# Norm chains between w_o and the feed-forward moved to the other half of PSUM, sums in two parts, two feed-forward chapters of h0 in a row

## The reference, cut to what matters

```python
y = hybrid_mixer(...)                      # its last step is  concat @ w_o
x = x + g1 * rms_norm_2(y, mix_post_g)     # "residual 3"
h = rms_norm_2(x, ffn_pre_g) * (1 + sc2) + sh2   # "apply 4"
g, u = split(h @ w_ffn_in)
y = (silu(g) * u) @ w_ffn_out              # D_FF = 2816 hidden channels
x = x + g2 * rms_norm_2(y, ffn_post_g)     # "residual 5"
```

## Time and profile before

| what | value |
|---|---|
| median of 3 runs | 2596.87 us (2590.79 to 2598.59) |
| the profiled execution's own time | 2598.15 us |
| its span | 2595.5 us (2.65 us lie around it) |
| mean granted TensorE clock | 0.946 of full speed |
| TensorE busy | 2337.8 us, 90% |
| VectorE, GpSimd, ScalarE busy | 1438.1, 1371.8, 819.5 us |

### The profile page before, as it was taken

One profiled execution on the slowest core, in us unless ns is written; L12 is line 12 of the kernel. 1 busy time (PEld: TensorE's weight loads), 2 busy tenths in 40 slices (PEclk: granted clock), 3 DMA queues, 4 the chain that ended last, 5 costly groups with the idle time before them and its releaser, 6 DMA issues. The chain is left out here.

```text
span 2595.5 us, 32228 instructions
## 1 busy us (share of the span) xinstructions
PE 2337.8 (90%) x11279; PEld 1926.6 (74%) x11279; DVE 1438.1 (55%) x2168; ACT 819.5 (32%) x1454; POOL 1371.8 (53%) x1332
## 2 busy tenths in 40 slices
PE   6898998999999999898788968797899999999995
PEld 2687888788887787776557846675678878888874
DVE  1743646577663999758789667648632212222236
ACT  3531113034213888623234257524320000000012
POOL 2545556652344887275369856575653833333360
PEclk9899999999998999898899979898999999999997
DMA  7435444423365565152223567452221311111121
GB/s 272 146 114 163 126 136 137 162 66 110 118 198 167 159 172 154 53 183 66 98 75 114 162 178 232 159 182 61 73 78 49 113 47 49 49 49 49 49 65 65
DMA packets 179725, 304.86 MB, mean 117 GB/s; under 512 B 34860, under 2 KB 73448, under 8 KB 178288
## 3 DMA queue, kind: packets, MB, share of 16 engines
q1 hardware_dynamic: 137760, 217.51, 28.9%
q10 hardware_dynamic: 41808, 85.31, 8.9%
HBM read 246.09 MB, written 56.66 MB: 117 GB/s over the span
## 5 line engine op out<-in xcount | busy, mean ns | idle before, releaser
L950 POOL TENSOR_SCALAR WH<-RAW 128x512 fp32r<-128x512 f32 (+1 forms) x462 | 344.2, 745 | 974.0 <-PE PS L1063 828.7
L1061 PE MATMUL PS<-HXH,WH 128*128 128x512 f32 (+1 forms) x1904 | 761.9, 400 | 74.5 <-ACT TM L1717 14.9
L1062 PE MATMUL PS<-HXL,WH 128*128 128x512 f32 (+1 forms) x1904 | 752.7, 395 | 0.0
L1063 PE MATMUL PS<-HXH,WL 128*128 128x512 f32 (+1 forms) x1904 | 751.6, 395 | 0.0
L953 POOL TENSOR_TENSOR WL<-RAW,WH 128x512 fp32r<-128x512 f32 (+1 forms) x462 | 632.1, 1368 | 38.5
L1061 PEld LDWEIGHTS PS<-HXH,WH 128*128 128x128 f32 (+1 forms) x1904 | 363.3, 191 | 161.9 <-issue 14.9
L1062 PEld LDWEIGHTS PS<-HXL,WH 128*128 128x128 f32 (+1 forms) x1904 | 363.5, 191 | 79.7 <-issue 3.8
L1063 PEld LDWEIGHTS PS<-HXH,WL 128*128 128x128 f32 (+1 forms) x1904 | 362.5, 190 | 79.5 <-issue 0.9
L2324 DVE TENSOR_TENSOR TM<-PS,TM 128x512 f32<-128x512 f32 x44 | 28.4, 686 | 378.7 <-ACT TM L1745 378.6
L1745 ACT ACTIVATE TM<-PS 128x512 f32<-128x512 f32 x44 | 23.9, 596 | 552.3 <-PE PS L1063 552.3
L1061 PE MATMUL PS<-AHH,WH 128*128 128x512 f32 x352 | 140.4, 399 | 24.1 <-DVE AHL L2328 20.4
(11 more groups left out here) (295 smaller groups left out, 4185.0 us busy)
## 6 DMA issues: line engine op xcount, KB each, us to landing
RAW<-in_ada_w SPq DMA_DIRECT2D x160, 256.0 KB, 2.9
RAW<-in_w_ffn_in SPq DMA_DIRECT2D x224, 128.0 KB, 2.1
RAW<-in_w_in_ab SPq DMA_DIRECT2D x88, 256.0 KB, 2.7
RAW<-in_w_in SPq DMA_DIRECT2D x56, 256.0 KB, 2.6
RAW<-in_w_ffn_out SPq DMA_DIRECT2D x52, 256.0 KB, 2.6
XR<-XX ACTq DMA_DIRECT2D x3, 4096.0 KB, 12.1
XX<-XR ACTq DMA_DIRECT2D x3, 4096.0 KB, 12.6
RAW<-in_w_in_c SPq DMA_DIRECT2D x40, 256.0 KB, 2.7
```

Of the source, the lines that this page charges most:

```text
L950: g.tensor_scalar(WH[:, sw, 0:m], RAW[:, r, 0:m], 1.0, 0.0, ALU.mult, ALU.add).then_inc(gpsimd_done, 1)
L1061: mm(out, wh, xh, start=first, stop=False, **kw)
L1062: mm(out, wh, xl, start=False, stop=False, **kw)
L1063: return mm(out, wl, xh, start=False, stop=last, **kw)
```

## The change

1. `plan()`: the sum of squares 3 is cut into halves of four k, each listed right behind the wo lin that makes these k; the second half, resid 3, sum(4,h0) and apply(4,h0) get a `home`, a stat whose PSUM set they use: banks 1 to 3 as their ring of scratch tiles, bank 0 for the reciprocal root. The set is freed only when the last step of the chain that lives there is done. Sum 4 and apply 4 of h1 have no home and stay in SBUF.
2. Apply 4 is cut: h0 into two halves around wo(1,h1), h1 into four pairs of k, one ahead of each fo lin of h0.
3. `midk`: stat 3 of both parts behind k=1, stat(4,h1) behind k=5.
4. Chapters 0 and 1: fi(0,h0), fi(1,h0), then the four fo lins of h0, then fi(0,h1), fi(1,h1) and the four fo lins of h1. The output weights of chapter 1 are loaded twice (4 more pieces of 256 KB, 4 more splits).
5. AHH/AHL: the halves go in turn to whichever (chapter, part) comes next.
6. A second sum tile SUM3 for sum 3.

```diff
+    def squares(n, p, half, home=None):
+        ev("sum", ("sum", n, p, half), n=n, part=p, ks=range(4 * half, 4 * half + 4), home=home)
+    def normed(p, x, ks, home=None):
+        ev("apply", ("apply", 4, p, x), n=4, part=p, ks=ks, home=home)
     for g, p in ((0, "h0"), (1, "h0"), (0, "h1"), (1, "h1")):
         w = weights("wo", g) if (g, p) != (0, "h0") else w_wo
         if (g, p) == (0, "h1"):
-            ev("sum", ("sum", 3, "h0"), n=3, part="h0")
             stats(3, "h0", mid=True)
-            ev("resid", ("resid", 3, "h0"), n=3, part="h0")
-            ev("sum", ("sum", 4, "h0"), n=4, part="h0")
+            ev("resid", ("resid", 3, "h0"), n=3, part="h0", home=("stat", 3, "h0"))
         if (g, p) == (1, "h1"):
             stats(4, "h0", mid=True)
-            ev("apply", ("apply", 4, "h0"), n=4, part="h0")
-        lin(("wo", g, p), "wo", g, p, w, last=True, midk=3,
+            normed("h0", 0, range(0, 4), home=("stat", 4, "h0"))
+        lin(("wo", g, p), "wo", g, p, w, last=True, midk=(1, 3)[g],
             mid={(0, "h1"): ("stat", 3, "h0"), (1, "h1"): ("stat", 4, "h0")}.get((g, p)))
-    ev("sum", ("sum", 3, "h1"), n=3, part="h1")
+        if (g, p) == (0, "h1"):
+            ev("sum", ("sum", 4, "h0"), n=4, part="h0", home=("stat", 4, "h0"))
+        if (g, p) == (1, "h1"):
+            normed("h0", 1, range(4, 8), home=("stat", 4, "h0"))
+        squares(3, p, g, home=("stat", 3, p) if g else None)
...
     stats(3, "h1", mid=True)
-    ev("resid", ("resid", 3, "h1"), n=3, part="h1")
-    hidden(0, "h0", w, mid=("stat", 3, "h1"), midk=3)
+    ev("resid", ("resid", 3, "h1"), n=3, part="h1", home=("stat", 3, "h1"))
+    hidden(0, "h0", w, mid=("stat", 3, "h1"), midk=1)
     ev("sum", ("sum", 4, "h1"), n=4, part="h1")
-    hidden_out(0, "h0", out_weights(0))
     w = weights("fi", 1)
     stats(4, "h1", mid=True)
-    ev("apply", ("apply", 4, "h1"), n=4, part="h1")
-    hidden(1, "h0", w, mid=("stat", 4, "h1"), midk=3)
-    hidden(0, "h1", weights("fi", 0))
-    hidden_out(0, "h1", out_weights(0))
-    hidden(1, "h1", weights("fi", 1))
-    w = out_weights(1)
-    for p in x2:
-        hidden_out(1, p, w, last=p == "h1")
+    hidden(1, "h0", w, mid=("stat", 4, "h1"), midk=5)
+    ws = [out_weights(0), out_weights(1)]
+    for x in range(4):
+        normed("h1", x, range(2 * x, 2 * x + 2))
+        hidden_out(x // 2, "h0", ws[x // 2], gs=(x % 2,))
+    for ch in range(2):
+        hidden(ch, "h1", weights("fi", ch))
+    for ch in range(2):
+        hidden_out(ch, "h1", out_weights(ch))
...
+        SUM3 = at("SUM3", [HALF], F32, HREG + 65536)
...
         def tm(name, i, w=HALF, p0=0, p1=P):
+            if name in HOME:
+                return bank(HOME[name], 1 + IN_HOME[HOME[name]].index((name, i)) % 3, w, p0, p1)
             return TM[TMAT[(name, i)] % 3][p0:p1, 0:w]
+
+        def home_before(name, i):
+            return prev[HOME[name]] if name in HOME and IN_HOME[HOME[name]].index((name, i)) < 3 else []
+
+        def rstd_of(n, part, w=HALF):
+            if ("stat", n, part) in IN_HOME:
+                return bank(("stat", n, part), 0, w)
+            return (RST0[part] if n == 0 else RST)[:, 0:w]
...
+        def aslice(ch, part):
+            o_ = HALF * (FI.index((ch, part)) % 2)
+            return slice(o_, o_ + PARTS[part][1])
...
-                        did(scalar_done, ("sqrt", n, part), ("free", nm))
+                        did(scalar_done, ("sqrt", n, part), *([] if nm in IN_HOME else [("free", nm)]))
...
-                        v.reciprocal(r_[:, 0:w], r_[:, 0:w]).then_inc(vector_done, 1)
+                        v.reciprocal(rstd_of(n, part, w), r_[:, 0:w]).then_inc(vector_done, 1)
...
-                        did(vector_done, ("H", "apply", n, part, k), ("tm", (name, k)))
+                        did(vector_done, ("H", "apply", n, part, k), ("tm", (name, i)), *([freed] if name in HOME else []))
...
-                        v.tensor_tensor(tm(name, k), ys(part, k), RST[:, :], ALU.mult).then_inc(vector_done, 1)
+                        v.tensor_tensor(tm(name, k, w), ys(part, k), rstd_of(n, part, w), ALU.mult).then_inc(vector_done, 1)
```

More of the change, by code:

```diff
@@ L334, in hidden, with hidden_out @@
         lin(("fi", ch, p), "fi", ch, p, w, last=last, **kw)
-    def hidden_out(ch, p, w, last=True):
-        for g in (0, 1):
+    def hidden_out(ch, p, w, last=True, gs=(0, 1)):
+        for g in gs:
             lin(("fo", ch, g, p), "fo", g, p, w[g], kts=2, last=last, h="A", ch=ch)
@@ L557, in program @@
             for n in ("rq_loaded", "g_loaded", "ot_stored", "nb_loaded"))
+        HOME = {e["name"]: e["home"] for e in TL if e.get("home")}
+        IN_HOME = {}
+        for e in TL:
+            if e["name"] in HOME:
+                IN_HOME.setdefault(HOME[e["name"]], []).extend((e["name"], i) for i in range(len(e.get("ks", range(KT)))))
         def uses(e):
@@ L564, in uses @@
                 return 2
+            if e["name"] in HOME:
+                return 0
+            if k in ("sum", "apply") and "ks" in e:
+                return len(e["ks"])
             if k in ("sum",):
@@ L591, in tm_before @@
         def tm_before(name, i):
+            if name in HOME:
+                ring = IN_HOME[HOME[name]]
+                n = ring.index((name, i))
+                return [ring[n - 3]] if n >= 3 else []
             n = TMAT[(name, i)]
@@ L728, in cols @@
             return PC[:, b + i:b + i + (n or m)]
+        FI = [(e["group"], e["part"]) for e in TL if e.get("layer") == "fi"]
+        def aslice(ch, part):
+            o_ = HALF * (FI.index((ch, part)) % 2)
+            return slice(o_, o_ + PARTS[part][1])
         def ada_acc(v, n, x):
@@ L1070, in stat @@
                     pe.wait_ge(*of("free", job_before))
-                mm(bank(name, 0, w), ONF[:, :], SUM[:, 0:w], start=True, stop=True).then_inc(products_done, 1)
+                mm(bank(name, 0, w), ONF[:, :], sum_of(n, part)[:, 0:w], start=True, stop=True).then_inc(products_done, 1)
                 did(products_done, ("job", name))
@@ L1168, in _ @@
                             pe.wait_ge(vector_done, upto("A", e["ch"], part, k))
-                            xh, xl = AHH[:, k, off:off + n], AHL[:, k, off:off + n]
+                            xh, xl = AHH[:, k, aslice(e["ch"], part)], AHL[:, k, aslice(e["ch"], part)]
                         f, l = k == 0, k == kts - 1
@@ L1534, in _ @@
                     w = PARTS[part][1]
-                    for k in range(KT):
+                    for i, k in enumerate(e.get("ks", range(KT))):
                         src = xs(part, k) if n in (0, 1, 2, 4) else ys(part, k)
@@ L1540, in _ @@
                             act.wait_ge(*of("X", n, part, k))
-                        for use_before in tm_before(name, k):
+                        for job_before in home_before(name, i):
+                            act.wait_ge(*of("free", job_before))
+                        for use_before in tm_before(name, i):
                             act.wait_ge(*of("tm", use_before))
-                        A(tm(name, k, w), src, ACT.Square).then_inc(scalar_done, 1)
+                        first = name in HOME and k == 0
+                        A(sum_of(n, part)[:, 0:w] if first else tm(name, i, w), src, ACT.Square).then_inc(scalar_done, 1)
                         did(scalar_done, ("sq", n, part, k))
@@ L1748, in _ @@
                             act.wait_ge(vector_done, upto("av", ch, part, j))
[L1749 to L1751 removed]
+                            at_ = FI.index((ch, part))
+                            if at_ >= 2:
+                                act.wait_ge(products_done, upto("job", ("fo", FI[at_ - 2][0], 1, FI[at_ - 2][1])))
+                            A(AHH[:, j, aslice(ch, part)], tm(name, j), ACT.Copy).then_inc(scalar_done, 1)
                             did(scalar_done, ("ahi", ch, part, j))
@@ L2129, in _ @@
                     w = PARTS[part][1]
-                    for k in range(1, KT):
+                    total = sum_of(n, part)[:, 0:w]
+                    for i, k in enumerate(e.get("ks", range(KT))):
+                        if k == 0:
+                            continue
                         dve.wait_ge(scalar_done, upto("sq", n, part, k))
-                        in1 = tm(name, 0, w) if k == 1 else SUM[:, 0:w]
-                        v.tensor_tensor(SUM[:, 0:w], tm(name, k, w), in1, ALU.add).then_inc(vector_done, 1)
+                        in1 = tm(name, 0, w) if k == 1 and name not in HOME else total
+                        v.tensor_tensor(total, tm(name, i, w), in1, ALU.add).then_inc(vector_done, 1)
                         did(vector_done, ("sum", n, part),
-                            ("tm", (name, k)), *([("tm", (name, 0))] if k == 1 else []))
+                            ("tm", (name, i)), *([("tm", (name, 0))] if k == 1 else []))
                         dve.wait_ge(vector_done, so_far(vector_done))
@@ L2327, in _ @@
```

(2 more changed lines are left out.)

31 lines of the change are left out of this document (19 added, 12 removed).

## The result

| | before | changed |
|---|---|---|
| median | 2595.69 us (4 runs, 2590.79 to 2598.59) | 2570.76 us (4 runs, 2567.49 to 2576.09) |
| ratio | | 0.9911, 95% interval 0.9898 to 0.9924 |
| span of the profiled execution | 2595.5 us | 2570.3 us |
| from the start of wo(0,h1) to that of fi(2,h0) | 219.7 us | 192.6 us |
| of which TensorE's work | 177.7 us | 177.7 us |

Faster by 24.9 us; the forecast was 28.4 (2568.5 us; the range was 2560 to 2584). The stretch that the change reorders is 27.1 us shorter, and what lies behind it 0.5 us. What lies ahead of it, where TensorE's work is as before, took 2.4 us longer in this execution.

The account below looks back on a forecast made before the run. Bound: TensorE, losing 42.0 us in the stretch to long norm chains and slow clock. Losses left 0.7 + 8.5 + 2.4 + 2.0 = 13.6 us, so 28.4 gained: 2568.5 us, own range 2563 to 2576, 8-in-10 range 2560 to 2584.

Parts of the forecast that it names:

- Sum 3 of h0: At the stat behind k=1 of wo(0,h1): SUM3 comes slightly late, loss 0.7 us, before 1.56.
- Resid 3 of h0: Ahead of wo(1,h1): 8 k in PSUM at 1.32 us each end as wo(0,h1) does; no loss, no margin.
- Stat(4,h0): Behind k=3 of wo(1,h1): sum 4 is ready at 1762.5, the stat due at 1764.6; the 10.39 us gap goes.
- Apply 4 of h0, late next: At fi(0,h0), whose set the chain holds to its last k: TensorE idle 8.5 us, plus 2.4 us slow clock.
- Resid 3 of h1, sum 4 of h1: Under fi(0,h0) and fi(1,h0): both chains hidden, sum 4 by 2 us; gaps of 8.14 and 9.95 us go.
- The fo lins: Pairs of apply k of h1 between fo lins of h0: 2 us of waits for sets, range 0 to 4.
- The pieces: Four more weight loads and splits, taken as hidden; as a rival, 10.9 us in the open, 2579, chance 0.12.
- The slower rival: GpSimd slows PSUM chains too, resid and apply at 2.72 us a k: 49 us lost, 2604, chance 0.07.
- The half case: Half the slower rival's slowdown, a k at about 2.0 us: some 17 us more lost, 2586, chance 0.07.
- One cause for all the gaps: In the reordered stretch: every TensorE gap comes from a norm chain too long for its covering lin; 42.0 us lost.
- Rows 8: Convolution profile: VectorE instructions with one SBUF, one PSUM input take 0.661 us, not slowed beside 17.67 us of GpSimd additions.

Follow-up runs that it names:

- the later stats: The changed kernel with stat 3 of both parts back behind k=3: 2582.21 us, ratio to the kernel before 0.9956.
- That kernel: The changed kernel with all scratch and roots in SBUF, each set still held to its chain's end: 2592.05 us, ratio to the kernel before 0.9992.
- Three of the edits: From the changed kernel: scratch back in SBUF, 2587.65 us; stats of sum 3 behind k=3, 2582.21 us; chapter order of before, 2575.22 us.
- the last kernel: Kernel with early release and fo lins first, plus second half of apply 4 of h0 in stat(3,h1)'s set, that stat behind k=2: 2559.43 us.

## Why the prediction was right, point by point

- *Sum 3 of h0:* 0.7 us forecast, 0.70 measured.
- *Resid 3 of h0:* 1.32 us a k taken, 1.26 measured; no gap, as forecast, and no margin, as the later stats showed. The convolution's instruction was the right neighbour; the page of the Trainium skill on the other side (Perfetto Trace Analysis, § Optimizing Scalar/DVE Operations), by which PSUM costs VectorE 65 ns more an instruction, does not show: 1.26 us a k against 1.27 us in quiet SBUF. The measurement decides.
- *Stat(4,h0):* no wait, as forecast.
- *Apply 4 of h0, late next:* the gap was put at 8.5 us and is 8.32. The slow clock behind it was put at 2.4 us and is 2.95. This and the 2.5 us at the fo lins are the terms that were put too low.
- *Resid 3 of h1, sum 4 of h1:* no gap, as forecast.
- *The fo lins:* 2 us forecast, 2.5 measured, in two places, both ended by the evictions that the prediction named.
- *The pieces:* hidden, as forecast. *The upstream:* 2.4 us of scatter ahead of the stretch, which no term had, are most of what is left between 28.4 and 25.2 us of span.
- *The slower rival* did not come about, since VectorE's PSUM instructions are not slowed; and where it was built, the price was too high by 12 us (2592 against 2604): its stretch loses 37.4 us, not 49. The gaps at wo(1,h1), fi(0,h0) and fi(1,h0) are 6.1, 10.7 and 6.0 us in place of 11.3, 16.8 and 10.0; against that, 3.2 are lost at stat(3,h0) in place of 0.7. A step was missing: a stall of TensorE silences GpSimd, whose weight slots no longer come free, and with it the contention. The rows for it lay open: the fast k at 1828 us in the earlier trace rows come right after GpSimd's last instruction in the earlier trace rows. The prediction used them only to name GpSimd, and did not ask why it had stopped. That kernel takes 2.7 us a k, where the prediction lets this rival decide from about 2.4, and is level with the kernel before. The half case was not built, and its price stays open.
- *One cause for all the gaps:* not so for the one of 3.01 us, nor for 4.4 of the 9.95, which come from the order of the chapters. The forecast had them gone by the right means all the same, since it took the new order for them.
- *Rows 8:* GpSimd's 17.67 us begin 1.93 us behind VectorE's start and outlast it, so it works beside 17.25 of the 19.18 us. The reading holds.

What the rule behind it says: the Trainium skill, SBUF — State Buffer, § SBUF: two separate sides, has VectorE and GpSimd share one pair of SBUF ports under an exclusive lock, and a VectorE instruction with two SBUF inputs takes part in it only against a GpSimd instruction that reads SBUF. The runs agree: 0.68 to 0.75 us with one SBUF input at all times, 0.9 to 1.8 with two where they fall on a GpSimd instruction, 0.68 to 0.74 where they do not.

What stays open: no run took back the halves of sum 3 or the two halves of apply 4 of h0 alone, so their share of the 9.6 us is not shown. Three of the edits, each taken back, lengthen the stretch by 17.5, 12.5 and 6.3 us, more together than the 27.1 gained, so they overlap and do not add. What the 5.3 us between a stat and its root, 3.35 of it the reciprocal, would give if they were shortened was not tried.

## What to carry to other kernels

Where an engine's chain runs beside GpSimd, count the SBUF tensors that each VectorE instruction reads: idle PSUM banks as scratch more than halved the time of a residual's k here (1.26 us against 2.72), at no price per instruction. A buffer lent out that way is held to the chain's end, so ask which lin wants it next. When a gap is closed, ask in the same breath which chain is late behind it: here the wait came back 12 us later, and only 1.3 us was gained. Price a slow chain with the stall that it causes: what contends with it may stop too.

## What the runs showed of the hardware that was not expected

- ScalarE's apply steps with scratch in PSUM repeat every 1.27 us, against 1.38 in SBUF, and 1.38 also where GpSimd leaves out its subtraction, so GpSimd is not the reason:

```profile
1775.78 0.74 ACT L1623 ACTIVATE PS<-PS,MOD,CO 128x512 f32<-128x512 f32 x1
1776.55 0.60 ACT L1631 ACTIVATE HXH<-PS 128x512 fp32r<-128x512 f32 x1
1777.05 0.74 ACT L1623 ACTIVATE PS<-PS,MOD,CO 128x512 f32<-128x512 f32 x1
```

- Gaps of 3 us can go either way with the clock. Behind the one of 2.90 us in the last kernel the granted clock of the next 5.3 us is 0.73 (between the levels of 1.2 and 2.4 GHz: part of it at each), and behind the one of 3.09 us in the kernel with scratch in SBUF it is 0.68. Behind the one of 3.01 us in the kernel before, the stretch 1895.5 to 1900.0 has 1.00, and so has the 5.2 us behind the same gap with the old order. The first two are followed by a stat, the other two by matmuls of a lin; whether that is the difference is not shown.
